# Issuing one matmul of each weight chunk as two over parts of its 256 columns

## The reference

```python
def swiglu(h, w_gate, w_up, w_down):                       # layers 0 and 1, D_FF = 2816
    return (jax.nn.silu(h @ w_gate) * (h @ w_up)) @ w_down
...
h = h + jnp.square(jax.nn.relu(u @ w_up[l])) @ w_down[l]   # layers 2 and 3, D_FF_2 = 4096
```

## Time and profile before

| what | value |
|---|---|
| median of 3 runs | 1875.36 us (1869.99 to 1878.12) |
| span of the profiled execution | 1875.1 us |
| PE busy | 1841.3 us (98%) in 15964 matmuls |
| PEld busy | 1750.7 us (93%) in 15964 weight loads |
| DVE, ACT, POOL busy | 1259.6, 956.6, 307.3 us |
| mean granted TensorE clock | 0.997 |

### The profile page before, as it was taken

How to read it: one execution, slowest core, us unless ns; L and a number is a source line. 1 busy time by engine, 2 the same in 40 slices (tenths; PEclk the granted TensorE clock), 3 DMA queues, 4 the chain that set the end, 5 groups by cost and what they waited for, 6 DMA issues and landing times.

```text
span 1875.1 us, 37406 instructions
## 1 busy us (share of the span) xinstructions
PE 1841.3 (98%) x15964; PEld 1750.7 (93%) x15964; DVE 1259.6 (67%) x1676; ACT 956.6 (51%) x1381; POOL 307.3 (16%) x176
## 2 busy tenths in 40 slices
PE   7999999999999999999999999999999999999998
PEld 7989998998888999999989999999999899999998
DVE  6884677665689557777648865676547785577643
ACT  5634466444563445554545455565434445555533
POOL 0050221000003212200002542310002352230000
PEclk9999999999999999999999999999999999999999
DMA  6443354656445334555656553456555663446652
GB/s 238 157 159 113 125 169 158 214 184 196 154 145 172 113 123 149 178 194 181 204 189 196 193 170 126 147 182 198 185 189 181 206 195 126 136 158 203 189 187 96
DMA packets 92165, 317.66 MB, mean 169 GB/s; under 512 B 11744, under 2 KB 12896, under 8 KB 91744
## 3 DMA queue, kind: packets, MB, share of 16 engines
q1 hardware_dynamic: 91424, 314.69, 51.7%
q10 hardware_dynamic: 576, 0.57, 0.1%
HBM read 305.00 MB, written 1.05 MB: 163 GB/s over the span
## 4 chain that ended last, share of the span: by engine, by line
PE 83%; DVE 12%; ACT 3%; issue 1%; DMA 1%; SPq 0%; DVEq 0%; ACTq 0%
PE bank L2007 82%; DVE wlo L1131 4%; DVE area L1131 3%; DVE area L1137 2%; ACT area L634 1%; ACT whi L640 1%; PE bank L2571 1%; DMA raw<-in_weights 1%; DVE hl L1137 1%; DVE xT L1137 1%; DVE area L1651 0%; DVE area L1649 0%; PE bank L2592 0%; ACT L622 0%; PE bank L2226 0%
## 5 line engine op out<-in xcount | busy, mean ns | idle before, releaser
L1131 DVE TENSOR_TENSOR wlo<-raw,whi 128x1024 fp32r<-128x1024 f32 x518 | 668.6, 1305 | 412.6 <-ACT whi L640 412.3
L2007 PE MATMUL bank<-hh,whi 128*128 128x256 f32 x2928 | 830.0, 284 | 18.5 <-DVE wlo L1131 15.9
L2007 PE MATMUL bank<-hh,wlo 128*128 128x256 f32 x2928 | 814.4, 279 | 0.0
L2007 PE MATMUL bank<-hl,whi 128*128 128x256 f32 x2928 | 807.2, 279 | 0.0
L640 ACT CAST whi<-raw 128x1024 fp32r<-128x1024 f32 x572 | 589.3, 1046 | 398.8 <-PE bank L2007 351.9
L2007 PEld LDWEIGHTS bank<-hh,whi 128*128 128x128 f32 x2928 | 551.3, 188 | 33.8 <-DVE wlo L1131 18.7
L2007 PEld LDWEIGHTS bank<-hl,whi 128*128 128x128 f32 x2928 | 551.1, 190 | 1.4 <-issue 1.4
L2007 PEld LDWEIGHTS bank<-hh,wlo 128*128 128x128 f32 x2928 | 551.4, 188 | 0.0
L1787 POOL TENSOR_TENSOR area<-area 128x512 f32<-128x512 f32 (+4 forms) x86 | 135.1, 1578 | 567.3 <-DVE area L1137 250.6
L1787 POOL TENSOR_TENSOR wlo<-raw,whi 128x1024 fp32r<-128x1024 f32 x54 | 133.9, 2481 | 384.7 <-ACT whi L640 384.7
L2007 PE MATMUL bank<-FH,whi 128*128 128x256 f32 x640 | 180.1, 281 | 0.0
(11 more groups left out here) (132 smaller groups left out, 1907.4 us busy)
## 6 DMA issues: line engine op xcount, KB each, us to landing
raw<-in_weights SPq DMA_DIRECT2D x572, 512.0 KB, 4.0
area<-area SPq DMA_DIRECT2D x96, 64.0 KB, 3.6
area<-area SPq DMA_DIRECT2D x16, 128.0 KB, 3.9
cst<-in_const SPq DMA_DIRECT2D x1, 1188.0 KB, 7.9
cst<-in_const SPq DMA_DIRECT2D x1, 1024.5 KB, 5.6
xT<-in_x SPq DMA_DIRECT2D x4, 256.0 KB, 7.9
out<-xT SPq DMA_DIRECT2D x4, 256.0 KB, 2.9
area<-in_lev SPq DMA_DIRECT2D x2, 384.0 KB, 6.8
```

Of the source, the lines that this page charges most:

```text
L1131: return v.tensor_tensor(dst, x, y, op)
L2007: return e.matmul(ps, x, y, start=start, stop=stop, skip_group_check=skip)
```

## The change

In six stages (`gu` of layers 0 and 1, `up` and `down` of layers 2 and 3) the third matmul of one block of a chunk, low weights by high activations, is issued as two, over columns 0 to n and n to 256, both with the same stationary block. The two write the parts of the same PSUM columns that the one wrote. `n` is 32, 128, 128, 64, 128 and 192 for the six stages. The block is the fifth of the chunk (`q == 4` or `m == 4`). In `project` the two chunks that are worked on together are left as they were; in `by_rows` the first chunk and the last two are.

```diff
+PARTED = {("gu", 0): 32, ("gu", 1): 128, ("up", 2): 128, ("up", 3): 64, ("down", 2): 128, ("down", 3): 192}
...
+            def mm3_parted(ps, i, at, xh, xl, n):
+
+                wh, wl = whi[:, i % RING, at:at + 128], wlo[:, i % RING, at:at + 128]
+                mm(ps, wh, xh, False, False, True)
+                mm(ps, wh, xl, False, False, True)
+                mm(ps[:, 0:n], wl, xh[:, 0:n], False, False, True)
+                return mm(ps[:, n:T], wl, xh[:, n:T], False, False, True)
...
-                            x = mm3(bank[b][:, (m - m0) * T:(m - m0 + 1) * T], i, 128 * q, xh[:, k, :], xl[:, k, :], k == 0, k == job.nk - 1)
+                            ps = bank[b][:, (m - m0) * T:(m - m0 + 1) * T]
+                            if q == 4 and (name, L) in PARTED:
+                                x = mm3_parted(ps, i, 128 * q, xh[:, k, :], xl[:, k, :], PARTED[name, L])
+                            else:
+                                x = mm3(ps, i, 128 * q, xh[:, k, :], xl[:, k, :], k == 0, k == job.nk - 1)
...
+                def parted(k, m, n):
+                    return mm3_parted(bank[m // 2][:, m % 2 * T:m % 2 * T + T], job.first + k, 128 * m, FH[:, k, :], FL[:, k, :], n)
+
                 for k in range(nk - TAIL):
...
-                        x = term(k, m)
+                        x = parted(k, m, PARTED[name, L]) if k and m == 4 and (name, L) in PARTED else term(k, m)
```

## The result

| | before | after |
|---|---|---|
| median, 14 runs each | 1875.82 us (1869.99 to 1882.19) | 1881.20 us (1878.55 to 1884.72) |
| ratio | | 1.0036 (95% interval 1.0024 to 1.0048) |
| span of the profiled execution | 1875.1 us | 1879.0 us |

The changed kernel is 5.4 us slower, where +6.7 us was forecast. The page of the changed kernel has the same picture as the earlier trace rows: 202 matmuls and loads more, and TensorE still makes most of the chain (84%).

What follows compares the result with a forecast made beforehand. TensorE, busy 98% of the span, was taken as the bound; +4.1 us (169 slow chunks) + 4.4 (33 fast) - 1.1 - 0.7 (unsplit matmuls behind) = +6.7 on the median of 1875.36, 1882 us; range 1874 to 1902 us.

Steps and rivals of the forecast that it cites:

- The pace: In the changed stages, 256-column matmuls run at 117.8 or 113.2 ns each, slow behind norm_sum, until a disturbance resets them.
- The fast pace in `gu` of layer 1: Last part of that stage: 113.2 ns a matmul, said to begin behind a pause of some 90 ns.
- The price of a piece: At each split matmul, each piece waits for its weight load, about 111 ns however narrow; 222 ns the pair.
- The rival in which pieces are priced by their columns: At each split, the second load takes no time, the pair some 120 ns: -13.9 us, 1861 us; chance 0.07.
- the one in which narrow pieces stream at the plain float32 rate: Pieces under 256 columns at 0.84 ns a column: 1888 us, or 1939 us with two records each; chance 0.10.
- The reset: Behind each split pair the stream settles at the fast 113.2 ns; slow chunks lose 24 ns, fast ones 134 ns.
- The settling: Five or six longer slots behind each pair, about 25 ns a chunk, bounded by 0 and 31.
- a draw of 82 in 107 as behind pauses: Of 107 pauses where the first matmul waited for weights, 82 settled at 113 ns, 25 at 118; taken as evidence for pairs.
- the wide second piece: In gu of layer 0, the second piece of 224 columns leaves hardly a gap, so the stream might stay slow.
- the rival with a chance of 0.33, a reset that fails: Two or more changed stages stay at 117.8 ns behind the pair: about +12 us for two, 1901 us for all; chance 0.33.
- The sum: Over the changed stages and what runs unsplit behind: 4.1 + 4.4 - 1.1 - 0.7 = +6.7 us.
- `gu` of layer 1, +2.8 instead of +3.7 us: In that stage, 15 slow chunks at 0.024 us and 25 fast ones at 0.134 us: +3.7 us.

Runs made afterwards that it cites:

- the first two experiments: Kernel before with one pair of halves per gu and up, in the chunk behind norm_sum (1859.0 us) or the last ahead of it (1878.98 us).
- the trace with more places: Kernel before with halves behind norm_sum in each gu, up and q2a, in chunk 24 of layer 1's gu and each wo's second chunk: 1859.26 us.
- the best kernel's trace: Kernel before with one pair of halves in each gu and up, in the first chunk behind norm_sum: 1859.0 us, ratio 0.9906.
- one run: Kernel before with one pair of 224 and 32 columns in each gu and up, behind norm_sum: 1871.72 us, ratio 0.9988.

## Why the prediction was right

*The pace.* That the stages ran at two paces, and that the slow one began behind `norm_sum`, was the step on which all else stood. The medians of the first two experiments show it: the same pair is worth 19 us (1878.25 to 1859.0 on one chip) one chunk behind `norm_sum` and nothing one chunk ahead of it; the trace with more places shows the pair at work in all four stages. Two readings under it were wrong, though the sum, which goes by windows, doesn't use them. The fast pace in `gu` of layer 1 didn't begin behind the pause of some 90 ns in the earlier trace rows: the loads are 113 ns apart already from 851.68 to 854.51 us, behind a wait of 0.33 us at 851.10. And `norm_sum` doesn't settle the stream slow as such; it swaps the pace that it meets. In the changed kernel it met a fast stream in all four stages, with split chunks ahead of it.

*The price of a piece.* 222 ns were forecast for the pair; measured are 108 and 111, 219 ns. Each piece of 8 to 224 columns took 108 to 112 ns, and a piece of 248 took 110 to 119, presumably because there the columns are the longer part. The rival in which pieces are priced by their columns is gone, and so is the one in which narrow pieces stream at the plain float32 rate, by which pieces of 32 and 224 would have cost 299 ns. All of this fits a piece that waits for its load. By the rule that the Trainium skill gives in TensorE: Matmul & The Clock Gate, section "Back-to-back issue gap", N / 2.4 + 2.5 ns, eight pieces of 32 would take an estimated 127 ns (200 ns by the least gap of some 25 ns that its table gives for up to 64 columns); the eight gaps between their loads are 0.90 us in sum. The section itself says that the rule leaves out the loads, and gives some 81 ns for a load with a matmul of 128 columns; halves took 108 to 111 ns here, so the trace disagrees with that figure too. In these traces, where each matmul has a load of its own, pieces of 8 to 224 columns cost the same, as they would if the load set the least distance.

*The reset.* It worked in every stage, from the first split chunk behind `norm_sum` on in `gu` and in `up` of layer 2, and from the second in `up` of layer 3. The settling was 25 ns by estimate; the chunks of 2847 ns leave 2847 - 222 - 2606 = 19, and those of 2860 leave 32. But the reason that the prediction gave, a draw of 82 in 107 as behind pauses, doesn't hold for the pairs. What a pair does depends on its widths and on the pace that it meets. Only six of the 202 pairs met a slow stream: five turned it, and one of 64 and 192, the first behind `norm_sum` in `up` of layer 3, kept it. All the others met a fast stream, and left it fast wherever it could be followed. Here the forecast had luck: it took one outcome for all widths, and nearly all the pairs that met a slow stream were of widths that turn it. In `gu` of layer 0 it hung on the order of the pieces. 32 and 224 turned the stream the one time that they met it slow; 224 and 32 kept it slow three times of three. The prediction had feared the wide second piece instead. With 248 and 8 the rival with a chance of 0.33, a reset that fails, would have come true: it kept the slow stream 28 times of 28.

*The sum.* The term that was off most is `gu` of layer 1, +2.8 instead of +3.7 us: 0.5 us of it is that the stage waited less for VectorE (1.1 us before, 0.6 after). `gu` of layer 0 was 0.4 us over, for pieces of 32 and 224 settle more slowly.

## What to carry to other kernels

A stream of matmuls can be several per cent off its best pace with every engine's busy share unchanged, and only the distance between starts shows it: compare the same instruction's pace in several stages before asking what bounds it. A repair that holds should be paid once, behind the event that spoils the stream, and not in each chunk: four pairs gained 0.9%, 202 lost 0.4%. Before crediting the repair, read the pace just ahead of it: in two of the four stages of the best kernel's trace the stream was fast already. And each piece of a split matmul, with its own load of 128 columns, took 108 ns or more here however narrow it was, so the split was not priced by columns.

## What the runs showed of the hardware that I had not expected

- fp32r matmuls of 256 columns run at 113.3 or 117.8 ns each and stay at either for over 1400 matmuls; with 512 columns it is about 229 or 233 ns.
- `norm_sum`'s two plain float32 matmuls swap the pace: fast to slow 37 times of 37, slow to fast 10 times of 11.
- What an fp32r matmul split over its columns does depends on the widths and their order. Halves gave fast 115 times of 115 that could be followed, 11 of them from the slow pace; 64 and 192 were fast behind it 29 times of 30 (one of two from the slow pace); 32 and 224 turned slow to fast once. Eight of 32, 248 and 8, and 224 and 32 kept the pace that they met (slow 39, 28 and 3 times). 8 and 248, and 96, 80 and 80, changed it in a round of three chunks. What in the array or its loads decides stays open; no run here tells it.
- The kernel before probably owes a part of its own spread (1860.54 to 1883.73 us beside one run) to this; that isn't shown by a trace of it.
